# The output stages of a long fused kernel, reordered by token tile, with rows loaded ahead and no barriers

## The reference, cut to what matters

```
h = h + mod[2] * rms_norm(y, norm_mix_post[i])        # y = mixer output @ w_out (+ b_out in layer 1)
v = rms_norm(h, norm_mlp_pre[i]) * (1 + mod[4]) + mod[3]
h = h + mod[5] * rms_norm(square(relu(v @ w_mlp_in[i])) @ w_mlp_out[i], norm_mlp_post[i])
# layer 1 begins with u = rms_norm(h, norm_mix_pre[1]) * (1 + mod[1]) + mod[0];  z = u @ hy_w_in + b_in
```

## Time and profile before

| | us |
|---|---|
| median of 3 runs | 3989.63 |
| lowest, highest | 3977.97, 3989.87 |
| the profiled execution: its own time | 3998.85 |
| its span, first to last instruction | 3997.1 |

### The profile page before, as it was taken

How to read it: one execution, slowest core, us unless ns; L and a number is a source line. 1 busy time by engine, 2 the same in 40 slices (tenths; PEclk the granted TensorE clock), 3 DMA queues, 4 the chain that set the end, 5 groups by cost and what they waited for, 6 DMA issues and landing times.

```text
span 3997.1 us, 31969 instructions
## 1 busy us (share of the span) xinstructions
PE 2892.8 (72%) x10786; PEld 1684.0 (42%) x10786; DVE 2728.8 (68%) x5411; ACT 745.7 (19%) x1497; POOL 940.1 (24%) x794
## 2 busy tenths in 40 slices
PE   7988598667888865578967666664570676968598
PEld 2956276224322222125735433111130544957296
DVE  2556978787767679667786578569979653555444
ACT  1311111111101001112013111001110342533153
POOL 0003223233323233343340133233445000000000
PEclk9998799778989887788978878876685787989799
DMA  7349799899999998999994599898999412543154
GB/s 251 127 160 373 296 365 371 324 371 373 392 388 395 383 354 299 373 384 345 384 396 156 191 367 372 352 361 344 354 407 393 161 42 86 191 176 142 58 173 143
DMA packets 277098, 1156.44 MB, mean 289 GB/s; under 512 B 19127, under 2 KB 19768, under 8 KB 178200
## 3 DMA queue, kind: packets, MB, share of 16 engines
q0 software_dynamic: 112768, 812.33, 51.2%
q1 hardware_dynamic: 162584, 336.37, 23.1%
q10 hardware_dynamic: 1600, 5.96, 0.4%
HBM read 1150.46 MB, written 4.13 MB: 289 GB/s over the span
## 4 chain that ended last, share of the span: by engine, by line
PE 44%; DVE 27%; DMA 22%; issue 4%; ACT 2%; POOL 1%; SPq 0%; DVEq 0%; POOLq 0%; ACTq 0%; PEldq 0%
DMA arena<-in_peer_uv,arena 10%; DMA ring<-in_w_mod 8%; DVE arena L2352 8%; PE ps L1137 7%; PE ps L866 5%; PE ps L747 5%; PE ps L749 5%; PE ps L748 5%; PE ps L1054 5%; DVE arena L2376 4%; PE ps L977 2%; PE ps L732 2%; PE ps L852 1%; PE ps L1101 1%; DVE w_lo L1928 1%
## 5 line engine op out<-in xcount | busy, mean ns | idle before, releaser
L2652 POOL DMA_INDIRECT arena<-in_peer_uv,arena x768 | 926.2, 1206 | 2160.2 <-PE ps L1137 960.1
L1137 PE MATMUL ps<-arena 128*128 128x512 f32 x1664 | 975.0, 725 | 485.5 <-DVE arena L2362 471.6
L1137 PEld LDWEIGHTS ps<-arena 128*128 128x128 f32 x1664 | 346.6, 223 | 1037.9 <-DVE arena L2362 650.3
L2352 DVE CUSTOM_DVE_ANT_0 arena<-arena,hA 128x1024 f32<-128x1024 f32 x512 | 614.8, 1221 | 206.6 <-DMA arena<-in_peer_uv,arena 201.2
L1617 ACT ACTIVATE arena<-arena 128x1 f32<-128x1 f32 x768 | 154.9, 203 | 2222.1 <-DVE arena L2352 2220.9
L2376 DVE SCALAR_TENSOR_TENSOR arena<-arena 128x1024 f32<-128x1024 f32 x345 | 441.2, 1279 | 3.9 <-DVE arena L2364 0.3
L2352 DVE CUSTOM_DVE_ANT_0 arena<-arena,hB 128x1024 f32<-128x1024 f32 x256 | 308.4, 1220 | 179.3 <-DMA arena<-in_peer_uv,arena 177.6
L866 PE MATMUL ps<-ring,condS 128*2 128x512 f32 x576 | 288.5, 648 | 122.0 <-DMA ring<-in_w_mod 119.7
L1928 DVE TENSOR_TENSOR w_lo<-ring,w_hi 128x1024 fp32r<-128x1024 f32 x220 | 264.0, 1222 | 159.6 <-ACT w_hi L1396 152.5
L747 PE MATMUL ps<-hT_hi,w_hi 128*128 128x256 f32 x992 | 285.8, 288 | 25.4 <-DVE hT_lo L1936 24.9
L749 PE MATMUL ps<-hT_hi,w_lo 128*128 128x256 f32 x992 | 283.5, 286 | 0.0
(11 more groups left out here) (314 smaller groups left out, 3449.3 us busy)
## 6 DMA issues: line engine op xcount, KB each, us to landing
ring<-in_w_mod SPq DMA_DIRECT2D x48, 2048.0 KB, 20.0
ring<-in_w_in SPq DMA_DIRECT2D x16, 2048.0 KB, 16.5
ring<-in_w_mlp_in SPq DMA_DIRECT2D x64, 512.0 KB, 5.9
ring<-in_w_mlp_out SPq DMA_DIRECT2D x64, 512.0 KB, 5.8
ring<-in_peer_wq SPq DMA_DIRECT2D x12, 2048.0 KB, 16.7
ring<-in_w_in SPq DMA_DIRECT2D x44, 512.0 KB, 5.9
vec<-mods SPq DMA_DIRECT2D x27, 512.0 KB, 8.2
ring<-in_w_out SPq DMA_DIRECT2D x6, 2048.0 KB, 8.7
```

The costliest lines, as they stand in the source:

```text
L1137: mm = pe.matmul(ps[:, 6 + c, :], uv[:, j % SLOTS, 0:P], uv[:, j % SLOTS, D + c * CW:D + (c + 1) * CW], start=start, stop=stop)
L2352: dve.tensor_tensor_reduce(row, row, peer_buf[p][:, t, :], 1.0, 0.0, ALU.mult, ALU.add, dots[:, column(j):column(j) + 1]).then_inc(dot_don ...
L2652: pool.indirect_dma_start(uv[:, j % SLOTS, :], None, A["peer_uv"], at).then_inc(uv_full[j % SLOTS], 16)
```

## The change

In the four output stages:

- The output layer is multiplied so that tile 0 is complete first (`out_tokens`, `down`). The down layer's chunks now alternate between the column halves; its last two chunks are multiplied for tile 0 both, then for tile 1 both, and are given back to the ring only then.
- Post and norm go tile by tile and read PSUM directly. ScalarE makes squares and root (`y_root_tile`, `x_root_tile`), VectorE the rest (`post_tile`, `next_norm_tile`). Both engines have one written order of these steps and of the quarters of the next layer's chunk 0 (`out_stage`).
- The post rows have buffers of their own (`post_row`, `post_full`, `post_used`), so SP issues them, the next norm's rows and the next weights without waiting for the residual; `n_h` is loaded ahead of the down weights.
- The next layer's chunk 0 is multiplied for tile 0, then for tile 1 (`split_features_tile`: 96 products of 128 columns each); the rest of the layer is written out and not looped.
- No barriers 1 to 4: GpSimd loads the Hyena tables after tile 0 of `L_ao`, the spectra after `L_down[0]`, and stores each tile of the result by itself.

```diff
-            return lambda c: v[c % 4, :, :, (c // 4) * CW:(c // 4 + 1) * CW]
+            return lambda c: v[c // 2, :, :, (c % 2) * CW:(c % 2 + 1) * CW]
...
+        STAGES = [(L_ao, "o_0", "n_m0", L_up[0]), (L_down[0], "m_0", "n_h", L_hin),
+                  (L_hout, "o_1", "n_m1", L_up[1]), (L_down[1], "m_1", None, None)]
+        def tile_banks(L, t):
+            return 2 * ((L.e0 + t) % 2)
...
+        POST_ROWS = ["o_0", "m_0", "o_1", "m_1"]
+        post_in = dict(zip(POST_ROWS, itertools.accumulate(16 * len(rows[name]) for name in POST_ROWS)))
...
+        def y_tile(k, t):
+            if k == 2:
+                return yH[:, t, :].rearrange("p (c f) -> p c f", c=2)
+            b = tile_banks(STAGES[k][0], t)
+            return ps[:, b:b + 2, :]
+        def y_junk(k, t):
+            return (Kf[:, 1] if k == 2 else cs)[:, t, :]
...
+                if name in POST_ROWS:
+                    if name != "o_0":
+                        sp.wait_ge(post_used, POST_ROWS.index(name))
+                    for row, src in rows[name]:
+                        sp.dma_start(post_row[row], src.partition_broadcast(P)).then_inc(post_full, 16)
                     return
...
             load_rows("m_0")
+            load_rows("n_h")
             weights(L_down[0])
-            load_rows("n_h")
...
-            def mlp(i):
-                turn_norm(f"n_m{i}")
-                features(L_up[i], hT)
+            def out_tokens(L):
+                for t in range(NT):
+                    for c in range(2):
+                        s = (L.g0 + c) % 2
+                        if t == 0:
+                            enter(L, c)
+                        if c == 0:
+                            pe.wait_ge(bank_free, L.e0 + t + 1)
+                        for k in range(KT):
+                            mm = pe.matmul(ps[:, tile_banks(L, t) + c, :], hT[:, k, t * P:(t + 1) * P], ring[:, s, k, :],
+                                           start=k == 0, stop=k == KT - 1)
+                        if t == NT - 1:
+                            mm.then_inc(ring_done, 1)
+                    if t == 0:
+                        mm.then_inc(y_mm, 1)
+            def down_part(L, c, t):
+                s, g = (L.g0 + c) % 2, c // 2
+                ts = slice(t * P, (t + 1) * P)
+                for k in range(KT):
+                    mm = split_products(ps[:, tile_banks(L, t) + c % 2, :], [x[:, KT * g + k, ts] for x in (hid_hi, hid_lo)],
+                                        [w[:, s, k, :] for w in (w_hi, w_lo)], g == 0 and k == 0, g == 3 and k == KT - 1)
+                return mm
+            def down(i):
                 L = L_down[i]
...
+                for c in range(6):
+                    enter(L, c)
+                    pe.wait_ge(hid, 8 * i + 2 * (c // 2) + 2)
+                    for t in range(NT):
+                        if c == 0:
+                            pe.wait_ge(bank_free, L.e0 + t + 1)
+                        mm = down_part(L, c, t)
+                    mm.then_inc(ring_done, 1)
+                enter(L, 6)
+                pe.wait_ge(hid, 8 * i + 8)
+                down_part(L, 6, 0)
+                enter(L, 7)
+                down_part(L, 7, 0).then_inc(y_mm, 1)
+                down_part(L, 6, 1).then_inc(ring_done, 1)
+                down_part(L, 7, 1).then_inc(ring_done, 1)
+            def split_features_tile(s, e, t):
+                ts = slice(t * P, (t + 1) * P)
+                for b in range(4):
+                    o = ps[:, 2 * (e % 2) + b // 2, (b % 2) * T + t * P:(b % 2) * T + (t + 1) * P]
+                    for k in range(KT):
+                        mm = split_products(o, [w[:, s, k, b * P:(b + 1) * P] for w in (w_hi, w_lo)],
+                                            [x[:, k, ts] for x in (hT_hi, hT_lo)], k == 0, k == KT - 1)
+                return mm
+            def tile_split(name, t):
+                tile_turned(name, t)
+                pe.wait_ge(tr_low, 4 * low_no[name] + 2 * t + 2)
+            def next_features(k):
+                L, _, name, N = STAGES[k]
+                turn_tile(name, hA, 0)
+                s = enter(N, 0, 0, N.e0)
+                tile_split(name, 0)
+                split_features_tile(s, N.e0, 0)
+                turn_tile(name, hA, 1)
+                tile_split(name, 1)
+                split_features_tile(s, N.e0, 1).then_inc(ring_done, 1)
+                turned(name)
+                features(N, hT, 1)
...
-            tokens(L_ao, hT)
-            wall_at(pe, 1)
-            mlp(0)
-            wall_at(pe, 2)
+            out_tokens(L_ao)
+            next_features(0)
+            down(0)
             pe.wait_ge(tab_in, 16 * (N_ATT_TABS + N_HY_TABS))
...
-            turn_norm("n_h")
-            features(L_hin, hT)
+            next_features(1)
             r = turn_no["vv"]
...
-            tokens(L_hout, hT)
-            wall_at(pe, 3)
-            mlp(1)
-            wall_at(pe, 4)
+            out_tokens(L_hout)
+            next_features(2)
+            down(1)
...
+            def y_root_tile(k, t):
+                L = STAGES[k][0]
+                if k == 2:
+                    act.wait_ge(y_sum, t + 1)
+                elif t == 0:
+                    act.wait_ge(y_mm, k + 1)
+                else:
+                    act.wait_ge(ring_done, L.g0 + L.n + 2)
+                st.do(act.activation(y_junk(k, t).rearrange("p (c f) -> p c f", c=2), y_tile(k, t), ACT.Square,
+                                     accum_out=stat[:, 2 + t:3 + t]))
+                st.settle()
+                act.activation(stat[:, 2 + t:3 + t], stat[:, 2 + t:3 + t], ACT.Sqrt, scale=1.0 / D,
+                               bias=eps[:, 0:1]).then_inc(y_root, 1)
+            def x_root_tile(k, t):
+                act.wait_ge(x_ready, NT * k + t + 1)
+                st.do(act.activation(y_junk(k, t), xs[:, t, :], ACT.Square, accum_out=stat[:, t:t + 1]))
+                st.settle()
+                act.activation(stat[:, t:t + 1], stat[:, t:t + 1], ACT.Sqrt, scale=1.0 / D,
+                               bias=eps[:, 0:1]).then_inc(x_root, 1)
...
+            def out_stage(k):
+                _, _, name, N = STAGES[k]
+                y_root_tile(k, 0)
+                if name is None:
+                    y_root_tile(k, 1)
+                    return
+                x_root_tile(k, 0)
+                split_high(N, 0, (0, 1, 2))
+                y_root_tile(k, 1)
+                turn_tile_high(name, 0)
+                split_high(N, 0, (3,))
+                x_root_tile(k, 1)
+                turn_tile_high(name, 1)
+                split_high(N, 1)
...
+                    split_high(L_down[i], c)
...
-            for c in range(2):
...
-            wall_at(act, 1)
+            out_stage(0)
             mlp(0)
-            wall_at(act, 2)
+            out_stage(1)
...
-            def post(name, y):
...
+            def add_out_bias(t):
+                L = STAGES[2][0]
+                if t == 0:
+                    dve.wait_ge(y_mm, 3)
+                else:
+                    dve.wait_ge(ring_done, L.g0 + L.n + 2)
+                b = tile_banks(L, t)
+                dve.tensor_tensor(y_tile(2, t), ps[:, b:b + 2, :], halves_of(post_row[SHIFT]), ALU.add).then_inc(bank_free, 1)
+                dve.wait_ge(bank_free, L.e0 + t + 3)
+                dve.sem_inc(y_sum, 1)
+            def post_tile(k, t):
+                L = STAGES[k][0]
+                if k == 2:
+                    add_out_bias(t)
+                dve.wait_ge(y_root, NT * k + t + 1)
+                st.do(dve.reciprocal(stat[:, 2 + t:3 + t], stat[:, 2 + t:3 + t]))
+                st.settle()
+                ins = dve.scalar_tensor_tensor(halves_of(hA[:, t, :]), y_tile(k, t), stat[:, 2 + t:3 + t],
+                                               halves_of(post_row[GAIN]), ALU.mult, ALU.mult)
+                if k != 2:
+                    ins.then_inc(bank_free, 1)
+                    dve.wait_ge(bank_free, L.e0 + t + 3)
+                else:
+                    st.do(ins)
+                    st.settle()
+                dve.tensor_tensor(xs[:, t, :], xs[:, t, :], hA[:, t, :], ALU.add).then_inc(x_ready, 1)
+            def next_norm_tile(k, t):
+                name = STAGES[k][2]
+                dve.wait_ge(x_root, NT * k + t + 1)
+                st.do(dve.reciprocal(stat[:, t:t + 1], stat[:, t:t + 1]))
+                st.settle()
+                st.do(dve.scalar_tensor_tensor(hA[:, t, :], xs[:, t, :], stat[:, t:t + 1], vec[:, SCALE, :], ALU.mult, ALU.mult))
+                st.settle()
+                dve.tensor_tensor(hA[:, t, :], hA[:, t, :], vec[:, SHIFT, :], ALU.add).then_inc(normed, 1)
+            def out_stage(k):
+                _, own, name, N = STAGES[k]
+                dve.wait_ge(post_full, post_in[own])
+                st.do(dve.tensor_tensor(post_row[GAIN], post_row[GAIN], post_row[GATE], ALU.mult))
+                st.settle()
```

(88 more changed lines are left out.)

56 lines of the change are left out of this document (10 added, 46 removed).

## The result

The changed kernel takes 4027.71 us (median; 4009.64 to 4033.31, 4 runs) against 3989.75 (3977.97 to 3991.35): slower, ratio 1.0094 with a 95% interval of 1.0055 to 1.0133. It was to be 3967.6. Both median and profile vary with the first 3300 us, which the change does not touch; the part that it touches, from the first product of the attention output layer to the end of the span, is the cleaner measure. Before: 3997.1-3312.9 = 684.2 us. After: 4007.9-3291.2 = 716.7 us, 32.5 more.

The account below looks back on a forecast made before the run. The prediction took dependency chains that stop TensorE in four output stages as the bound. Gains and losses of 13.4+2.8+7.4-0.7-1 = 22 us brought 3989.6 to 3967.6, own range 3954 to 3982, 8-in-10 range 3936 to 3996.

Parts of the forecast that it names:

- the price of the small product: Next layer's chunk 0: a split product with 128 columns was taken to cost 0.112 us, between 0.059 and 0.224.
- after a restart some 4.6 us go at half rate, so 13.0: Tile 0 of chunk 0: 96 products cost 10.8 us warm, but 13.0 us when begun after a stop.
- the prediction's other estimate: Chunk 0 by the skill page's 81 ns a product: two tiles some 18.5 us, whole change 38 us, near 3952.
- forecast +13.4: First output stage: tile 0 starts early and chunk 0 ends at 3377.9 instead of 3391.3, a gain of 13.4 us.
- forecast +2.8: Second output stage: the down layer ends 7.9 us later, yet chunk 0 ends sooner, a gain of 2.8 us.
- forecast +7.4: Third output stage, with its bias added on VectorE first: chunk 0 ends at 3803.1 instead of 3810.5, gaining 7.4 us.
- forecast -0.7: Last output stage: stall and restart delay the layer, the shorter tail ends at 3997.8, a loss of 0.7 us.
- the 1 us for rows: Before the first down layer: the next norm's three rows, sent ahead of its weights, may delay these by 1 us.
- The stall before chunk 7: Down layers: TensorE waits 5.5 us for chunk 7's weights and restarts cold, so the layer ends 7.9 us later.
- C: Rival for chunk 0: the split form at 128 columns runs like f32, 0.224 a product; 4032, slower; chance 15%.
- A: Rival for chunk 0: small products are cheap, gain 53 to 38 us, 3937 to 3952; chance 15%.
- B: Rival at stage starts: first weights come late, each start moves 3.5 to 5 us, gain 7 to 11, about 3981; chance 15%.

Follow-up runs that it names:

- price: Changed kernel with idle product streams of one form each, begun at full clock, behind its last layer; 128-column split products stepped by 0.111 us.
- late_post: Changed kernel with chunk 0 whole, down layers in ring order, and tile 0's post waiting for its output layer's end; 3956.86 us, ratio 0.9946 to before.
- cold: Changed kernel with chunk 0 whole and down layers in ring order, plus idle streams after pauses behind its last layer; 192 products of 128 columns took 41.23 us.

## Why the prediction was wrong

**The step that failed** is in the price of the small product, and not in its row: "after a restart some 4.6 us go at half rate, so 13.0." I had taken the length of a restart from streams of other forms and put it under this one. At full clock the product costs 0.111, as good as my 0.112; after a stop it costs 0.216, because the clock does not come back under it, for both tiles. Two tiles cost 20.7+20.7 instead of 13.0+10.8, 17.7 us more a stage, and the restart that I thought paid there is paid again at chunk 1, 2.3 us. Three stages: 60 us. A smaller slip: by my own steps the 81 ns of the prediction's other estimate give 17.8 us for two tiles and a gain of 40, where it says 18.5 and 38.

**What this does to the sum**, by intervals from one chunk 1 to the next. Start of `L_ao` to chunk 1: before 3377.70+13.6-3312.91 = 78.4, after 80.6, a loss of 2.2; forecast +13.4, with the correction -4.3. To the next: 216.6 and 237.2, a loss of 20.6; forecast +2.8, corrected -17.2. To the third: 202.6 and 210.4, a loss of 7.8; forecast +7.4, corrected -12.6. To the end: 186.6 and 188.5, a loss of 1.9; forecast -0.7, corrected -3.0. With the 1 us for rows it is -38, measured -32.5. The first interval is 2 us better since `L_ao` kept a high clock in this profile (27.7 us; 30.0 before, the first 4.6 of them at 0.50). The 3.4 us of the second lie in the layers: from chunk 1 to the end of the down layer TensorE waited for low weights four times besides the stall, 4.9 us in all, where before it had waited 0.96 us. The first of the four:

```profile
3398.29 0.39 PE L780 MATMUL ps<-hT_hi,w_hi 128*128 128x256 f32 x1 [1.58 <-DVE w_lo L2045]
```

Why the weights came later is open. The 4.8 us of the third lie from `L_hin`'s end to `L_hout`'s end, mostly the convolution, which the change leaves alone. Here this part in before, in the changed kernel, and in price, which runs the changed kernel's code there:

```profile
3664.40:3765.60 101.20, 68.38 (x176) 37.04 (x176) 27.38 (x30) 7.71 (x10) 0.00 (x0) 0.81 0.06 21
3668.50:3764.40 95.90, 63.05 (x178) 35.62 (x179) 37.03 (x39) 12.61 (x18) 0.00 (x0) 0.86 0.16 59
3679.60:3778.60 99.00, 66.15 (x179) 36.56 (x179) 36.60 (x39) 12.72 (x18) 0.00 (x0) 0.81 0.16 57
```

Six of the profiled kernels have a mean granted clock of 0.81 there and take 98.9 to 101.2 us, the changed kernel and late_post have 0.86 and take 95.9 and 96.0. So at least 3 of the 4.8 us are the clock of this one profile.

**Right:** the stops. Tile 0 was to start 8.5, 9.8 and 11.0 us after its output layer, and did after about 8.2, 9.0 and 10.4. The row loads and barriers left the path. The stall before chunk 7 was 5.11 us in both down layers (5.5 and about 5 forecast), with a restart behind it at 0.43 a product for some 3 us, and its removal gave 7.7 and 6.8 us against my 7.9.

**Rivals.** C gave the right sign and, by luck, nearly the right time (4032 against 4027.71), by the wrong mechanism: a price of 0.224 at any clock. Price and cold refute it as put. A fell with price: halving the columns bought 0.008 us of 0.119. B fell: the third quarter was split 8.1 to 8.6 us after its slot came free, 8.6 forecast.

**Load time and busy time.** The Trainium skill, "TensorE: Matmul & The Clock Gate", section "LDWEIGHTS (loading the stationary operand)", says that the load takes time by its columns and not by its rows of contraction; 0.111 for 128 and 0.060 for 64 columns agree with the first half, and the second was not tried. The Trainium skill's section "Why this matters for your kernels" on the same page advises to keep TensorE busy continuously in order to reach the full clock. The first stream of cold was busy for 41 us without a pause and stayed at 1.2 GHz, so here the measurement differs. The 81 ns of the Trainium skill's "Back-to-back issue gap", which I had weighed, were not reached by any stream with 128 stationary columns; the best was 0.111 us.

## What to carry to other kernels

Here cutting a product's moving columns from 256 to 128 saved 0.008 us of 0.119, since the weight load stayed, and after a stop TensorE went at half clock for as long as the small products lasted. Price such a stream at the clock that it will start with, and begin it behind wide products. Giving up the order of a two-slot ring for an early first half cost a stall of a load less half a chunk and a restart, 7.7 and 6.8 us in the two down layers, and the stops were no shorter for it (97.1 and 97.4 us). The gain of tile by tile lay in post, norm and turn beside the output layer (28 us of stops in four stages); rows ahead, no barriers and the rest of the change gave 29 more together. None of it needed the next layer to be cut.

## What the runs showed of the hardware that I had not expected

- The granted clock depends on its own past: 192 identical products ran at 1.00 throughout when they began there (price, 0.111 us each) and at 0.50 throughout when they began after a pause (cold, 41.23 us for 192, 0.214 each).
- At full clock in the split form, 128 and 192 moving columns cost the same, 0.111 us, and 256 cost 0.119 (price); in cold, after a pause, the clock rose under the stream of 192 columns and not under that of 128.
- Idle products in TensorE's stops (8 or 10 and 2, f32, 512 columns) were worth 49 us in the changed kernel. In the one with whole chunks the last part fell by 8 us, of which the stops show 4.
- With the same code, the part from `L_hin`'s end to `L_hout`'s end took 95.9 us at a mean granted clock of 0.86 (changed) and 99.0 at 0.81 (price): one profile's clock is worth several us in a part that no edit touches.
